# A decoder trunk whose Strassen-like products put the high and low token halves into one matmul of 512 columns

## The reference, cut to what matters

```
hn = rms_norm(h)                                    # h: (528, 2048)
xa, sa, vb, gb, sb, ma, mb = split(hn @ w_in)       # w_in: 2048 x 14336
ya = rg_lru(conv4(xa)) * silu(sa)
pa = ya @ w_proj_a
yb = silu(layer_norm(conv31(vb * sigmoid(gb)))) * silu(sb)
pb = yb @ w_proj_b
h  = h + (sigmoid(ma) * pa + sigmoid(mb) * pb) @ w_out
out = rms_norm(h)[16:]
```

## Time and profile before

| what | value |
|---|---|
| median of 3 runs | 1776.68 us (1776.1 to 1776.89) |
| profiled execution | 1777.52 us |
| its span | 1775.7 us |
| PE busy | 1754.6 us (99%), 12812 matmuls |
| DVE busy | 1255.2 us (71%) |
| ACT busy | 839.8 us (47%) |
| DMA | 311.80 MB, mean 176 GB/s |

### The profile page before, as it was taken

The page is one execution under the profiler, slowest core; times in us unless marked ns, Lnnn a source line. Parts: engine busy times, 40 slices in busy tenths (PEclk is TensorE's granted clock), DMA queues, the critical chain, the costliest instruction groups (busy, mean ns, idle before and its releaser), DMA issues.

```text
span 1775.7 us, 30385 instructions
## 1 busy us (share of the span) xinstructions
PE 1754.6 (99%) x12812; PEld 1672.8 (94%) x12812; DVE 1255.2 (71%) x1489; ACT 839.8 (47%) x1142; POOL 298.0 (17%) x331
## 2 busy tenths in 40 slices
PE   9899999999999999999999999999999999999998
PEld 8899999999999988999999999999888899997886
DVE  7969988888888898777767667787633286764431
ACT  6556556455564523455555444555422154443322
POOL 0502222222122101111111111221100111120000
PEclk9999999999999999999999999999999999999999
DMA  6247867668677565777765767685767689757422
GB/s 207 88 125 157 189 162 172 154 150 182 156 162 167 137 184 166 190 208 220 205 173 156 191 167 203 179 214 165 234 213 243 174 213 202 178 139 265 154 83 95
DMA packets 285671, 311.80 MB, mean 176 GB/s; under 512 B 9440, under 2 KB 239968, under 8 KB 284384
## 3 DMA queue, kind: packets, MB, share of 16 engines
q1 hardware_dynamic: 211024, 188.21, 33.6%
q0 software_dynamic: 74512, 121.65, 31.6%
HBM read 235.38 MB, written 45.09 MB: 158 GB/s over the span
## 4 chain that ended last, share of the span: by engine, by line
PE 92%; DVE 3%; DMA 2%; ACT 1%; issue 1%; SPq 0%; POOL 0%; DVEq 0%; POOLq 0%; ACTq 0%
PE psum L793 39%; PE psum L886 28%; PE psum L753 16%; PE psum L980 7%; PE psum L994 3%; PE psum L853 1%; DMA t_lo<-m_spill 1%; DVE region L1914 1%; DMA raw<-in_w_proj_a 1%; DMA region<-in_x_channels 1%; DVE region L1545 0%; DVE w_lo L1699 0%; DVE t_lo L1830 0%; DVE total L1587 0%; DVE c_lo L1560 0%
## 5 line engine op out<-in xcount | busy, mean ns | idle before, releaser
L1224 ACT ACTIVATE w_hi<-raw 128x1024 fp32r<-128x1024 f32 x110 | 116.2, 1057 | 286.6 <-PE psum L753 134.7
L1479 DVE SCALAR_TENSOR_TENSOR region<-region,params 128x512 f32<-128x512 f32 x368 | 250.4, 743 | 0.0
L1699 DVE TENSOR_TENSOR w_lo<-raw,w_hi 128x1024 fp32r<-128x1024 f32 x110 | 134.7, 1226 | 131.7 <-ACT w_hi L1224 131.6
L1706 DVE TENSOR_TENSOR w_lo<-region,w_hi 128x1024 fp32r<-128x1024 f32 x108 | 132.2, 1224 | 103.0 <-ACT w_hi L1240 102.8
L1706 DVE TENSOR_TENSOR x_lo<-region,x_hi 128x1024 fp32r<-128x1024 f32 x108 | 132.0, 1224 | 89.8 <-ACT x_hi L1240 87.9
L886 PE MATMUL psum<-x_hi,w_hi 128*128 128x264 f32 x896 | 181.9, 284 | 0.0
L886 PE MATMUL psum<-x_lo,w_hi 128*128 128x264 f32 x896 | 181.9, 284 | 0.0
L793 PE MATMUL psum<-t_hi,w_hi 128*128 128x256 f32 x576 | 142.0, 285 | 0.0
L793 PE MATMUL psum<-t_lo,w_hi 128*128 128x256 f32 x576 | 141.3, 284 | 0.0
L793 PE MATMUL psum<-t_hi,x_hi 128*128 128x256 f32 x576 | 139.4, 281 | 0.9 <-ACT aux L1282 0.9
L793 PE MATMUL psum<-t_lo,x_hi 128*128 128x256 f32 x576 | 139.2, 281 | 0.0
(11 more groups left out here) (249 smaller groups left out, 4484.2 us busy)
## 6 DMA issues: line engine op xcount, KB each, us to landing
raw<-in_w_in SPq DMA_DIRECT2D x112, 512.0 KB, 4.0
region<-in_w_in SPq DMA_DIRECT2D x56, 1024.0 KB, 7.1
wide<-region POOLq DMA_DIRECT2D x98, 256.0 KB, 4.9
region<-in_w_proj_b SPq DMA_DIRECT2D x16, 1024.0 KB, 9.3
raw<-in_w_out SPq DMA_DIRECT2D x32, 512.0 KB, 3.7
raw<-in_w_proj_a SPq DMA_DIRECT2D x31, 512.0 KB, 4.2
region<-in_w_in POOLq DMA_DIRECT2D x28, 512.0 KB, 7.2
sigmoid_spill<-wide POOLq DMA_DIRECT2D x16, 512.0 KB, 5.4
```

Source lines behind the costliest of these rows:

```text
L1224: act.activation(cut_at(n)[0], raw_at(n).rearrange("p (k n) -> p k n", k=4), ACT.Copy).then_inc(hi_ready, 1)
L1479: ins = dve.scalar_tensor_tensor(conv_b[:, t, :], moved, w, conv_b[:, t, :], ALU.mult, ALU.add)
L1699: dve.tensor_tensor(lo, raw_at(n).rearrange("p (k n) -> p k n", k=4), hi.bitcast(F32), ALU.subtract).then_inc(lo_ready, 1)
L1706: dve.tensor_tensor(lo, operand_source(v, q).rearrange("p (r h) n -> p r h n", h=2), hi.bitcast(F32), ALU.subtract).then_inc(lo_ready, 1)
```

## The change

It does four things. A product becomes 8 matmuls of 512 columns (token high part and low part side by side, as an access pattern of two segments, into the two halves of a bank) and 8 of 256. All reads of the banks take 512 columns. The two halves are added where results leave: `join_first` for c11 and c21, after ACT has copied the upper halves (`copy_first`), and `join_rest` for c12 and c22 from the wider u2 and u3; the gate of all four is then one instruction over the slot. Third, `scale_ln` and `silu_ln` run under sa's units; POOL stores the finished pair to DRAM (`store_ln`), waits until the store has landed and loads the next, and under sb only `gate_yb` is left, on a reloaded pair. Fourth, the waits follow: `first_ready` and `rest_ready` stand for the four old ones.

```
-        x_hi, x_lo = sb("x_hi", [P, CT, T], F32R), sb("x_lo", [P, CT, T], F32R)
-        t_hi, t_lo = sb("t_hi", [P, 4, KH, HS], F32R), sb("t_lo", [P, 4, KH, HS], F32R)
+        x_parts, t_parts = sb("x_parts", [P, 2, CT, T], F32R), sb("t_parts", [P, 2, 4, KH, HS], F32R)
+        x_hi, x_lo = (x_parts[:, n] for n in range(2))
...
-        aux = sb("aux", [P, 2 * HS + 2 * SEQ])
-        u2, u3 = (aux[:, n * HS:(n + 1) * HS] for n in range(2))
-        ln = aux[:, 2 * HS:].rearrange("p (t s) -> p t s", t=2)
+        aux = sb("aux", [P, 4 * SEQ])
+        u2, u3 = (aux[:, n * SEQ:(n + 1) * SEQ] for n in range(2))
+        ln = aux[:, 2 * SEQ:].rearrange("p (t s) -> p t s", t=2)
...
+            def store_ln(i):
+
+                pool.wait_ge(ln_silu, 2 * i + 2)
+                pool.dma_start(pair_rows(conv_spill, i), ln).then_inc(ln_stored, 16)
...
                 spill_o(w)
-                if kind == SA and i < PAIRS - 1:
-                    load_h(i + 1)
+                if kind == SA:
+                    if i < PAIRS - 1:
+                        load_h(i + 1)
+                    store_ln(i)
+                    pool.wait_ge(ln_stored, 16 * (i + 1))
+                    load_ln(conv_spill, (i + 1) % PAIRS)
                 elif kind == SB:
...
+                for k in range(KH):
+                    pe.matmul(psum[:, bank, :].rearrange("p (a n) -> p a n", a=2), hi[:, k // 2, k % 2, :],
+                              parts[:, :, k, :], start=not more and k == 0, stop=False, skip_group_check=True)
                 pe.wait_ge(lo_ready, n + 1)
-                passes(lo, (0,), False, True).then_inc(multiplied, 1)
+                for k in range(KH):
+                    last = pe.matmul(psum[:, bank, 0:HS], lo[:, k // 2, k % 2, :], parts[:, 0, k, :],
+                                     start=False, stop=k == KH - 1, skip_group_check=True)
+                last.then_inc(multiplied, 1)
...
-            def gate_c11(v):
-
-                w = w_of(v)
-                act.wait_ge(multiplied, chunk(v, A12) + 1)
-                wait(act, o_spilled[w % 2], spills(w))
-                act.activation(o_slots[:, w % 2, 0, 0:HS], bank(v, 0), gate_of(v)).then_inc(c11_ready, 1)
-
-            def gate_c21(v):
+            def copy_first(v):
 
                 w = w_of(v)
                 act.wait_ge(multiplied, chunk(v, A22) + 1)
                 wait(act, o_spilled[w % 2], spills(w))
-                act.activation(o_slots[:, w % 2, 1, 0:HS], bank(v, 1), gate_of(v)).then_inc(c21_ready, 1)
-
-            def gate_rest(v):
-
+                b = 3 * (w % 2)
+                act.activation(o_slots[:, w % 2, :, 0:HS], psum[:, b:b + 2, HS:], ACT.Copy).then_inc(first_copied, 1)
+
+            def gate(v):
 
                 w = w_of(v)
                 if w < PA * PAIRS:
-                    act.wait_ge(c22_ready, v + 1)
-                    act.wait_ge(c12_ready, v + 1)
-                    rest = o_slots[:, w % 2, :, HS:]
+                    act.wait_ge(first_ready, v + 1)
+                    act.wait_ge(rest_ready, v + 1)
                     done = {MA: o_gated, MB: o_gated, SA: sa_silu, SB: sb_silu}[w // PAIRS]
-                    act.activation(rest, rest, gate_of(v)).then_inc(done, 1)
+                    act.activation(o_slots[:, w % 2], o_slots[:, w % 2], gate_of(v)).then_inc(done, 1)
...
-                        if SB * PAIRS < w_of(v) < PA * PAIRS:
-                            silu_ln(w_of(v) - SB * PAIRS - 1)
-                    if p == 6:
-                        gate_c11(v)
+                        if SA * PAIRS < w_of(v) <= SB * PAIRS:
+                            silu_ln(w_of(v) - SA * PAIRS - 1)
...
             def read_c22(v):
 
-                w = w_of(v)
                 dve.wait_ge(u3_ready, v + 1)
                 dve.wait_ge(multiplied, chunk(v, S1) + 1)
-                wait(dve, o_spilled[w % 2], spills(w))
-                dve.tensor_tensor(o_slots[:, w % 2, 1, HS:], u3, bank(v, 2), ALU.subtract).then_inc(c22_ready, 1)
+                dve.tensor_tensor(u3, u3, psum[:, 3 * (w_of(v) % 2) + 2, :], ALU.subtract).then_inc(c22_ready, 1)
 
             def read_c12(v):
 
-                w = w_of(v)
                 dve.wait_ge(multiplied, chunk(v, S4) + 1)
                 dve.wait_ge(u2_ready, v + 1)
-                dve.tensor_tensor(o_slots[:, w % 2, 0, HS:], u2, bank(v, 2), ALU.add).then_inc(c12_ready, 1)
+                dve.tensor_tensor(u2, u2, psum[:, 3 * (w_of(v) % 2) + 2, :], ALU.add).then_inc(c12_ready, 1)
+
+            def join_first(v):
+
+                first, b = o_slots[:, w_of(v) % 2, :, 0:HS], 3 * (w_of(v) % 2)
+                dve.wait_ge(first_copied, v + 1)
+                dve.tensor_tensor(first, first, psum[:, b:b + 2, 0:HS], ALU.add).then_inc(first_ready, 1)
+
+            def join_rest(v):
+
+                w = w_of(v)
+                dve.wait_ge(c12_ready, v + 1)
+                dve.wait_ge(c22_ready, v + 1)
+                wait(dve, o_spilled[w % 2], spills(w))
+                parts = aux[:, 0:2 * SEQ].rearrange("p (b a n) -> p b a n", b=2, a=2)
+                dve.tensor_tensor(o_slots[:, w % 2, :, HS:], parts[:, :, 0, :], parts[:, :, 1, :], ALU.add)\
+                    .then_inc(rest_ready, 1)
...
                         read_c12(v - 1)
+                        join_first(v - 1)
+                        join_rest(v - 1)
...
-                    if p == 3 and 0 <= i < PAIRS:
-                        scale_ln(i)
+                    if p == 3 and 0 <= i_sa < PAIRS:
+                        scale_ln(i_sa)
...
             read_u3(NV - 1)
+            copy_first(NV - 1)
...
-                if i == 1:
-                    gate_c21(NV - 1)
...
             read_c22(NV - 1)
+            join_first(NV - 1)
...
                     read_c12(NV - 1)
+                    join_rest(NV - 1)
                     gate_pb(NV - 1)
```

More of the change, by code:

```diff
@@ L381, in token_operand, with token_parts @@
             return [part[:, b] for part in (t_hi, t_lo)]
+        def token_parts(q):
+            if q in (A11, A12, S4):
+                k, t = (0 if q == A11 else KH), META + (HS if q == S4 else 0)
+                return x_parts[:, :, k:k + KH, t:t + HS]
+            return t_parts[:, :, {S1: T_N1, S2: T_T2, S3: T_T3, A22: T_T4}[q]]
         def spilled_block(q):
@@ L785, in product @@
                 hi, lo = cut_slots(slot(n))
-                operand = token_operand(q)
+                parts = token_parts(q)
                 if v == NX:
                     pe.wait_ge(operand_lo, SWITCH_ORDER.index(q) + 1)
[L790 to L796, removed]
                 pe.wait_ge(hi_ready, n + 1)
-                passes(hi, (0, 1), not more, False)
+                for k in range(KH):
+                    pe.matmul(psum[:, bank, :].rearrange("p (a n) -> p a n", a=2), hi[:, k // 2, k % 2, :],
+                              parts[:, :, k, :], start=not more and k == 0, stop=False, skip_group_check=True)
                 pe.wait_ge(lo_ready, n + 1)
-                passes(lo, (0,), False, True).then_inc(multiplied, 1)
+                for k in range(KH):
+                    last = pe.matmul(psum[:, bank, 0:HS], lo[:, k // 2, k % 2, :], parts[:, 0, k, :],
+                                     start=False, stop=k == KH - 1, skip_group_check=True)
+                last.then_inc(multiplied, 1)
             def bank_of(v, n):
@@ L945, in _ @@
                 if i == 0:
[L946 to L947 removed]
+                    pe.wait_ge(first_ready, NX - 1)
                 elif i == 1:
@@ L950, in _ @@
                 elif i in (2, 3):
-                    for done in (c11_ready, c21_ready, c12_ready, c22_ready):
+                    for done in (first_ready, c12_ready, c22_ready):
                         pe.wait_ge(done, NX)
@@ L967, in _ @@
                 if n < 2:
-                    for done in ((c11_ready,) if n == 0 else (c21_ready, c12_ready)):
-                        pe.wait_ge(done, NV)
+                    pe.wait_ge(first_ready if n == 0 else c12_ready, NV)
                 for g in range(8):
@@ L1274, in read_u2 @@
                 act.wait_ge(multiplied, chunk(v, S2) + 1)
-                wait(act, c12_ready, v)
+                wait(act, rest_ready, v)
                 act.activation(u2, bank(v, 1), ACT.Copy, scale=-1.0).then_inc(u2_ready, 1)
@@ L1396, in _ @@
                 if m == 0:
-                    gate_c21(NX - 1)
+                    copy_first(NX - 1)
                 if m == 2:
-                    gate_rest(NX - 1)
-                    silu_ln(PAIRS - 1)
+                    gate(NX - 1)
                 if m in (14, 18, 22):
@@ L1814, in gate_pb @@
                 i, w = v - NX, w_of(v)
-                dve.wait_ge(ln_loaded, 16 * (3 * PAIRS + i + 1))
-                for done in (c11_ready, c21_ready, c12_ready):
+                dve.wait_ge(ln_loaded, 16 * (4 * PAIRS + i + 1))
+                for done in (first_ready, rest_ready):
                     dve.wait_ge(done, v + 1)
```

39 lines of the change are left out of this document (17 added, 22 removed).

## The result

The changed kernel takes 1785.81 us (median of 5 runs, 1783.81 to 1787.17) against 1776.89 us for the kernel before (5 runs, 1776.10 to 1777.41): 1.005 times as long, 95% interval 1.0035 to 1.0065, so slower by 8.9 us. The profiled execution spans 1784.0 us against 1775.7.

A forecast was written before the change was run, and what follows sets the result against it. PE, busy 99% of 1775.7 us, was taken as the bound. Terms −17.8 + 10.4 + 1.0 − 1.3 + 2.6 + 0.4 = −4.7 us gave 1772.0 us as median, range 1758 to 1790.

The forecast's parts named there:

- the loop: Under sa, scale, SiLU, gate, spill, store to DRAM, reload into the same buffer: period 8.2 + X + Y against a 19.43 us unit.
- products, 36 units: 252 products, 16 matmuls of 256 columns replaced by 8 of 512 in each: −17.8 us, a unit 19.43 us.
- stall under sa: PE stops because the scale comes later each unit and c22 is read late: 7L − 81, +10.4 us (0 to 29).
- ma and mb: LN's existing loop there grows by 2.1 us and drifts 0.32 past the unit: +1.0 us (0 to 1.6).
- switch: At the switch to w_proj_a PE's 1.32 us stop behind the last scale and SiLU goes: −1.3 us (0 to −1.3).
- end: End of the units: copy before w_out's first cut, c12's read and join delay the last gate: +2.6 us (0.9 to 3.5).
- waits for u3: Last unit of each series, no product between S3 and A22: u3's wider read adds 0.2 us each, +0.4 us.
- X: Landing time of ln's store to DRAM under sa, third in the queue: 7.8 us, at least 6.5, up to 9.6.
- Y: Landing time of ln's reload under sa: 3.2 us alone, 6.1 shared with half the weights, taken as about 5.3.
- L: X + Y, store and reload landings under sa: 13.1 us taken, from 9.7 to 15.7; no stall below 11.6.
- Rival 3: Two segments cost as two matmuls: product gain zero, unit 19.93 us, 1785 us in all; chance 10%.
- The point of decision: The L from which the loop under sa eats the whole gain: 13.8 us, a stall of 15.1 us.

The follow-up runs named there:

- store first: The changed kernel, but POOL issues ln's store ahead of the spill and waits for it behind h's load: 1766.04 us, 0.9941 of the kernel before.
- LN alone: The kernel before with its 256-column products, only scale, SiLU, store and reload of ln moved under sa: 1788.9 us, 1.0070 of the kernel before.
- weights held back: The changed kernel, but under sa SP issues the second half of a unit's weights only once ln's store has landed: 1778.43 us, ratio 1.0012.
- last tail kernel: The new products with LN's scale and SiLU left under sb, plus the reordered end of the last unit: 1763.47 us, ratio 0.9931.

## Why the prediction was wrong

The working of the loop was right to some 3 us, and the size of one transfer in it was not. The products gave less than forecast too; with their −17.8 us in full the change would still have been slower than before.

| Term | predicted us | measured us | shown by |
|---|---|---|---|
| products, 36 units | −17.8 (19.43 each) | −14.1 (19.54 each) | spacing of the seeds |
| stall under sa | +10.4 | +19.7 | 195.56 − 9 × 19.54 |
| ma and mb | +1.0 | 0 | spacing 19.54 throughout |
| sb | 0 | 0 | no wait of PE |
| switch | −1.3 | −1.3 | stop of the earlier trace rows gone, stream unbroken from 1260.79 |
| end | +2.6 | +3.1, then 0.15 | starts 1569.89 to 1615.66 |
| waits for u3 | +0.4 | +0.5 | 1.4 us in two places (store first) for 0.9 |
| sum | −4.7 | +8.0 (span: +8.3) | |

**The step that failed is X, the landing of the store.** I took 7.8 us between 6.5 and 9.6, and it was 8.6 to 10.6, mean 9.5: the end of my own bound. Y was 4.6 where I took 5.3, so L is 14.1 and not 13.1. The multiplier is 7, so 1.0 us of landing is 7 us of time. By the formula with a unit of 19.54 (7L − 82) the stall is 16.6; measured are 19.7. (The forecast's own 7 × 13.1 − 81 is 10.7; its 10.4 comes with the unrounded 81.3.) The other kernels fit about as well: LN alone, L = 13.9 and a unit of 19.93, 11.7 by formula and 12.7 measured; weights held back, L = 13.2, 10.5 and 12.6; store first, hidden, 0 and 0. Scale to scale the rule 8.2 + L gives 22.3, and seven periods have a mean of 22.64. Two of the 3 us more are six periods of 0.34 over the rule; the last one isn't taken apart. L = 14.1 and 19.7 us are still within the bounds that the forecast had set for its own case (14.4 and 20), so those bounds didn't tell the two cases apart: what made it slower than before was this stall and the smaller product gain together. PE stops for u3 as well as for c22 (L807 waits for L1294, then for L1737), a second place of the same stop that I didn't name.

**Why X was too small.** I had the shared cost of a transfer from h's load (6.0 in the earlier trace rows) and made the store's from it by half rates. But the store stands with both h's load and SP's 1 MB in flight, from the first unit of sa on: the eight stores take 9.4, 9.1, 10.6, 9.3, 10.5, 9.0, 9.2 and 8.6 us (the last without h's load). Held apart from the weights it takes 6.2 us, alone 3.2. I treated the landing as a property of the transfer, when it is one of the moment: the same store, issued ahead of the gate, lands in 3.2.
The Trainium skill ("DMA: Bandwidth & Descriptors", Anatomy of one DMA) gives a fixed 2.0 us plus bytes over 436 GB/s, by which an estimate for this transfer is 3.2 us. The runs agree with it where the store is alone (3.2 in the earlier trace rows and with the store first) and take two to three times as long where it isn't (6.2, and 8.6 to 10.6).

**Where the store is issued decides X.** The working has the store "at gate + 3.0 at the earliest", behind two issues that it doesn't depend on, while SiLU has ended 2.8 us after the scale. That the place was the change's own was right; that L depends on it, and isn't an unknown beside it, is what I missed.

**Products.** On t the 512 columns took 230 ns and not 227: 8 × 3 ns × 144 = 3.5 us of the 3.7 missed. On x eight took 1.85 to 1.86 us, some 232 ns each against 230.4. Rival 3 is false: the units are 19.54 and not 19.93, and one segment gives no more than two.

**What went as reckoned.** Nothing waits under sb, DVE isn't the bound in any stage, the joins are hidden by the products' lead (store first, no stop of PE in a unit but 1.4 us at u3, in the same two places as the earlier trace rows), the stop at the switch goes (but it goes without the move of LN too, so the reason given for it isn't shown). At the end PE's stop went from 2.9 to 4.6 us plus one of 1.3, and the term was right to 0.6.

**The clock.** The working held that single stops of 1.3 to 2 us leave the clock alone. Most did; the one of 1.59 us under sa and the one of 1.97 us in the last tail kernel did not. What the first of them cost isn't taken apart: the stop for c22 that every neighbouring unit has is missing in that unit.

**The point of decision** was put at L = 13.8. It lies lower for the real product gain: −14.1 − 1.3 + 3.1 + 0.4 = −11.9, and 7L − 82 reaches that at L = 13.4.

## What to carry to other kernels

A loop through DRAM costs its landings once per iteration, and an error of 1 us in one landing is as many us as there are late iterations: size it by transfers that were in flight beside it, and look first at what it waits behind on the issuing queue. Issue a store as soon as its data are ready and wait for it as late as possible: here that order alone is worth 19.8 us, and makes a loss of 0.5% a gain of 0.6%. The effects of two parts of one change don't add up where one of them makes a loop the bound: take such a change apart before it is judged.

## What the runs showed of the hardware

- The same 512 KB store of POOL's queue lands in 3.2 us alone, 6.2 behind a spill and h's load, and 8.6 to 10.6 with 1 MB of SP's queue in flight as well.
- POOL's transfers overlap: with the store first, h's load (8.4 us), the reload (8.8) and a22's load (11.5), issued within 1.5 us and with 1 MB of SP's queue beside them, are all in flight together, and the store ahead of them lands in 3.2.
- A moving operand in two segments costs the same as one on the t operands (19.54 us per unit in both), and so does one stretch at an odd or an even place; 512 columns cost some 228 to 234 ns in a unit (1.82 to 1.87 us for eight), also with two banks or with weights used twice.
- The length of a stop of PE alone doesn't tell whether the clock falls: one of 2.11 us left it at 1.00, one of 1.97 was followed by 0.72 over 6 us; under sa one of 1.58 us left eight matmuls at 2.11 us, one of 1.59 was followed by eight in 3.64.
